# Context tokens of the input projection multiplied in plain float32 from the unsplit weights

## What is computed

```python
hc = modulate(rms_norm(ctx, norm1_g[l]), csh1, csc1)
out_c, ctx_states = mixer_block(hc, lp, (zero_state, zero_state), not last)
hx = modulate(rms_norm(x, norm1_g[l]), sh1, sc1)
out_x, _ = mixer_block(hx, lp, ctx_states, True)
...
def mixer_block(h, lp, init, need_output):
    cb, cc, cx, r, k, v, w_lo, a_lo, g_lo = split_proj(h @ lp["w_in"])
    y, finals = rwkv_scans(r, k, v, w_lo, a_lo, lp, init)
    if not need_output:
        return None, finals
```

## Time and profile before

| | us |
|---|---|
| median of 3 runs | 1660.35 |
| lowest and highest | 1658.63, 1661.67 |
| profiled execution, first to last instruction | 1657.6 |
| TensorE busy in it | 1571.5 |

### The profile page before, as it was taken

How to read it: one execution, slowest core, us unless ns; L and a number is a source line. 1 busy time by engine, 2 the same in 40 slices (tenths; PEclk the granted TensorE clock), 3 DMA queues, 4 the chain that set the end, 5 groups by cost and what they waited for, 6 DMA issues and landing times.

```text
span 1657.6 us, 36556 instructions
## 1 busy us (share of the span) xinstructions
PE 1571.5 (95%) x15540; PEld 1324.2 (80%) x15540; DVE 885.0 (53%) x1417; ACT 572.7 (35%) x987; POOL 219.5 (13%) x230
## 2 busy tenths in 40 slices
PE   7899998999999978999999999999979999999997
PEld 3787886999999766778777887777867788888886
DVE  1624213665566445888887224667454556555222
ACT  3422334332232223434443223535544222323221
POOL 0000002333233010111111121000001011111111
PEclk8899997999999988999999998999979999999999
DMA  8242100332210121222222232221102222222221
GB/s 340 77 147 77 51 26 8 99 106 92 81 42 4 53 77 52 98 79 102 101 81 107 88 104 76 82 79 57 46 26 98 80 93 86 100 101 95 90 102 68
DMA packets 38750, 139.74 MB, mean 84 GB/s; under 512 B 3040, under 2 KB 3552, under 8 KB 38112
## 3 DMA queue, kind: packets, MB, share of 16 engines
q1 hardware_dynamic: 38480, 135.76, 23.4%
q10 hardware_dynamic: 144, 2.10, 0.3%
HBM read 135.75 MB, written 2.10 MB: 83 GB/s over the span
## 4 chain that ended last, share of the span: by engine, by line
PE 86%; DVE 8%; ACT 3%; issue 1%; DMA 0%; POOL 0%; DVEq 0%; SPq 0%; ACTq 0%
PE bank L647 58%; PE bank L780 12%; DVE ffn_sb L2471 2%; PE bank L657 2%; PE bank L967 1%; PE bank L610 1%; PE bank L886 1%; PE bank L908 1%; PE bank L888 1%; PE bank L592 1%; PE bank L1285 1%; PE bank L910 1%; ACT arena L1752 1%; DVE w_in L2091 1%; PE bank L1256 1%
## 5 line engine op out<-in xcount | busy, mean ns | idle before, releaser
L647 PE MATMUL bank<-hf_hi,w_up 128*128 128x512 f32 x1376 | 424.9, 390 | 0.0
L647 PEld LDWEIGHTS bank<-hf_hi,w_up 128*128 128x128 f32 x1376 | 259.1, 188 | 53.6
L647 PE MATMUL bank<-hf_lo,w_up 128*128 128x512 f32 x688 | 271.2, 394 | 4.8 <-DVE w_up L2091 4.3
L647 PE MATMUL bank<-act_hi,w_down 128*128 128x512 f32 x704 | 216.8, 389 | 0.0
L780 PE MATMUL bank<-arena 64*64 64x32 f32 (+2 forms) x4992 | 177.0, 227 | 8.5 <-POOL arena L1930 7.6
L780 PEld LDWEIGHTS bank<-arena 64*64 64x64 f32 x4992 | 170.6, 137 | 13.2 <-issue 8.7
L1403 ACT ACTIVATE w_up<-ring 128x1024 fp32r<-128x1024 f32 x88 | 93.0, 1058 | 215.9 <-PE bank L647 215.9
L2091 DVE TENSOR_TENSOR w_up<-ring,w_up 128x1024 fp32r<-128x1024 f32 x88 | 108.0, 1229 | 105.3 <-ACT w_up L1403 105.2
L647 PEld LDWEIGHTS bank<-hf_lo,w_up 128*128 128x128 f32 x688 | 129.5, 188 | 39.4 <-DVE w_up L2091 13.2
L2471 DVE SCALAR_TENSOR_TENSOR ffn_sb<-ffn_sb 128x512 f32<-128x512 f32 x176 | 151.5, 861 | 5.5
L647 PEld LDWEIGHTS bank<-act_hi,w_down 128*128 128x128 f32 x704 | 132.2, 188 | 27.4
(11 more groups left out here) (319 smaller groups left out, 2364.8 us busy)
## 6 DMA issues: line engine op xcount, KB each, us to landing
ring<-w SPq DMA_DIRECT2D x76, 1024.0 KB, 4.7
ring<-w SPq DMA_DIRECT2D x32, 704.0 KB, 4.0
ring<-w SPq DMA_DIRECT2D x64, 256.0 KB, 2.9
arena<-w SPq DMA_DIRECT2D x2, 3072.0 KB, 22.6
x<-xT SPq DMA_DIRECT2D x1, 2048.0 KB, 11.8
arena<-w SPq DMA_DIRECT2D x2, 1024.0 KB, 20.3
x<-xT ACTq DMA_DIRECT2D x1, 2048.0 KB, 8.9
outT<-x SPq DMA_DIRECT2D x4, 512.0 KB, 2.7
```

Of the source, the lines that this page charges most:

```text
L647: ins = mm(out, w[:, a, k, :], of_block(b, k0 + k), start=first and k == 0 and m == 0, stop=last and k == n - 1 and m == 2)
```

## The change

The context is not split any more. VectorE scales the eight blocks into `hc` in place, ScalarE adds the shift in place (`shifted`) and itself signals `normed`. The nine context products are `whole_product`: eight plain float32 multiplications of 128x256, with the weights taken from the ring's unsplit copy. As TensorE now reads the ring, the slots of `W_INB` and `W_INC` may be loaded over only when the last product of the slot is done: `HELD` gives them `product` in place of `w_lo` in `FREED`. The split of the weights stays, as the x products of the same slots use it; so do all other products.

```diff
+HELD = ("W_INB", "W_INC")
...
+        if _name in WHOLE + HELD:
+            FREED.append(("product", DONE[len(FREED)]))
+        else:
             FREED.append(("w_lo", _n))
-        else:
-            FREED.append(("product", DONE[len(FREED)]))
...
-        hc_ = low_high("hc", at_n + KB * TX, at_s + KB * TX, KB, TC)
...
+            def whole_product(out, w, act):
+
+                for k in range(KB):
+                    ins = mm(out, w[:, k, :], act[:, k, :], start=k == 0, stop=k == KB - 1)
+                ins.then_inc(s["product"], 1)
...
-                        split_product(banks[(base + q * u + c) % (2 * q)][:, 0:t], w_of[name][blk], KB, hi, lo, 0, True, True)
+                        out = banks[(base + q * u + c) % (2 * q)][:, 0:t]
+                        if parts is hc:
+                            whole_product(out, slot_view(SLOT[name] + 2 * i + u)[:, KB * blk:KB * blk + KB, :], hc)
+                        else:
+                            split_product(out, w_of[name][blk], KB, *parts, 0, True, True)
...
-            stage("W_INB", [(0, hx, TX), (1, hx, TX), (1, hc_, TC)], 16)
+            stage("W_INB", [(0, hx, TX), (1, hx, TX), (1, hc, TC)], 16)
...
-            stage("W_INC", [(0, hx, TX), (0, hc_, TC), (1, hx, TX), (1, hc_, TC)], 19, before_last=head_sums)
+            stage("W_INC", [(0, hx, TX), (0, hc, TC), (1, hx, TX), (1, hc, TC)], 19, before_last=head_sums)
...
+            def shifted(shift, whole):
+
+                for k in range(KB):
+                    se.wait_ge(s["h_f"], split_n[0] + k + 1)
+                    act_f(whole[:, k, :], whole[:, k, :], ACT.Identity, bias=shift[:, k:k + 1]).then_inc(s["normed"], 1)
+                split_n[0] += KB
...
-            split_normed(mod[:, 0:8, 1], hc_[0], hc)
+            shifted(mod[:, 0:8, 1], hc)
...
-            norm_split(gains[:, 1], mod[:, 0:8, 1], hc, ctx_sb, rstd_c[:, :], hc_)
+            for k in range(KB):
+                V.scalar_tensor_tensor(hc[:, k, :], ctx_sb[:, k, :], gains[:, 1, k:k + 1], rstd_c[:, :], ALU.mult,
+                                       ALU.mult).then_inc(s["h_f"], 1)
```

More of the change, by code:

```diff
@@ L679, in body @@
                         return
-                    for c, (blk, (hi, lo), t) in enumerate(prods):
+                    for c, (blk, parts, t) in enumerate(prods):
                         pe.wait_ge(s["w_lo"], 4 * i + n0 + 2 * u + blk + 1)
```

## The result

The changed kernel's median is 1664.86 us (1660.42 to 1675.76, 20 runs), that of the kernel before, run beside it, 1659.69 us (1653.61 to 1665.61, 20 runs). The ratio is 1.0041, with a 95% interval of 1.0024 to 1.0057: slower, by 6.8 us from the ratio (4.0 to 9.5), 5.2 from the medians. The prediction said +5.5.

The account below looks back on a forecast made before the run. TensorE was taken to bound the input projection. Nine context products at +0.61 us each gave +5.5 us, VectorE's saving and the ring 0, so 1660.35 became 1665.9 us, with a range of 1662.3 to 1669.2.

Parts of the forecast that it names:

- TensorE bounds the stage: Input projection: TensorE runs its products almost without a hole, so a microsecond more of TensorE is a microsecond more of the whole.
- a sign of being wrong: Behind the input projection: the prediction counts as wrong if what follows the stage does not shift as a block.
- The old product, 2.87 us: Context product before the change: 24 records at 0.1195 us between starts, 0.3586 us a block, 2.87 us for 8 blocks.
- The new product, 3.43 to 3.52 with 3.48 taken: Plain context product, priced from lines 802 and 1049: 0.61 us more than the old, +5.5 us for nine.
- An entry price on top, up to 1.8 us: Start of each plain context product: possibly 0.1 us extra, 0.9 for nine, 1.8 if doubled for a way out.
- VectorE's saving worth 0: VectorE loses eight subtractions while TensorE runs 76.47 us without a wait; the saving was put at 0 us.
- The ring hold worth 0: Ring loads behind W_INB and W_INC wait for the slot's last product; landings of 2.5 to 5.3 us stay covered, 0 us.
- The clock, 1.7 us either way: Two half-clock stretches, after the hole at 155.38 and the head sums: one may be missed or met, 1.7 us either way.
- Four full passes: Rival on the plain product: four passes at the old 0.1195 us each, 3.82 us a product, +8.6 us; chance 0.05.
- Weight loads set the price: Rival on the context products: 0.1195 us is a weight load's price, 16 loads replace 24, -8.6 us; chance 0.04.

## Why the prediction was right

- **TensorE bounds the stage.** Right: the stage grew by the products' 5.2 us, and with a third of the context records gone it shrank by 8.59. What follows did not shift as a block all the way, though, which the prediction named as a sign of being wrong: 6.0 us at `ADA2`, 9.0 at line 1060, 4.9 at the end. The kernel with the longer hold alone, whose stage costs nothing more, scatters there as well (566.40 in place of 564.01 for the records of line 1049, and a span 0.5 us longer), so that sign asked for more than two single profiles can tell. That the span's 4.9 lies near 5.2 is luck in part.
- **The old product, 2.87 us.** Right: 8.59 / 9 = 0.954 for eight records is 0.119 each.
- **The new product, 3.43 to 3.52 with 3.48 taken.** 3.45 measured. The half of line 1049's spacing (0.2144) was a little low and line 802's rounded 0.22 a little high; the truth is 0.2156. The sum came to 5.2 for 5.5.
- **An entry price on top, up to 1.8 us.** There is none: the doubled product shows the second eight at 3.46. The late first start in line 802 does not come back in this stream.
- **VectorE's saving worth 0.** Right as far as the runs can tell: with the work put back TensorE has no new wait and the whole time is the same. The stage's agreement to 0.04 us is chance.
- **The ring hold worth 0.** Right: done alone it leaves the stage at 171.36 us for 171.31.
- **The clock, 1.7 us either way.** The stretches stayed, in 160.00 to 164.00 and around 220 us, and cost about the same: the x products behind the hole and behind the head sums took 7.37 and 7.36 us where a product takes 5.45, 1.9 us each. That such a stretch can be missed or met is seen where VectorE's work was put back: 1.6 us more at one place and 1.6 less at the other. The size of the scatter was low: the head sums alone differ by 2.8 us between two executions.
- **Four full passes** (+8.6). The count fits, as four turns of the columns are 0.427 of the 0.431 us, and the price of one is wrong: 0.1195 is a reduced record with its surplus of 0.013, and a plain multiplication has two records, not four, with next to none. 0.431 is four times 0.108.
- **Weight loads set the price** (-8.6). Half of it may be true. At 128 columns both formats stand at a floor of 0.111 us a record, which fits a weight load, and the old product at 256 columns is just above it. But the plain record at 256 is well over the floor, so having 16 loads in place of 24 buys nothing.

## What to carry to other kernels

With weights of 128x128, three multiplications in the reduced format beat one plain float32 multiplication at 256 columns, 0.359 against 0.431 us. At 128 columns the floor of 0.111 us a record turns it round: a product in two runs took 5.31 us in the reduced format and 3.57 in the plain one. So where tokens are few the plain form is the one to try; where between 128 and 256 columns the two meet was not measured. Price such an exchange by the distance of starts in a running stream of the same width, not by the mean length of a record. Check it in the stage that was changed, not in the difference of two whole spans. And look at what the bounding engine waits for between stages: here waiting for all banks where one was wanted cost as much as the whole change.

## What the runs showed of the hardware that was not expected

A record of 128 columns costs 0.111 us in the reduced format and 0.1116 in the plain one, 93% of what a reduced record of 256 columns costs (0.1195). Halving the columns in two runs therefore made a reduced product 5.31 us instead of 2.87, and a plain one only 3.57 instead of 3.45. The rows of before did not show a floor so near the old price: the head sums in them, 6.92 us for 48 records, ran at half clock in part. At a granted clock of 0.97 they take 0.110 us a record with two columns, so the floor does not depend on the columns. That it is the weight load fits, and was not shown apart from other things that each record has once. Records with narrower weights are shorter, as line 789 with weights of 128x64 and 128 columns in the chain of before, 0.061 us each:

```profile
239.30 1.46 PE bank L789 x24
```

That fits a price of the weights' width as well, but it lies under the 0.107 us of twice the columns too. These multiplications write to one half of the partitions and then the other, so they are no clean test, and what is said above of floor and columns holds for weights of 128x128. The surplus of 0.013 us that a reduced record has above its columns at 256 and at 512 is not explained by any run here.

Besides the stretch at the head sums, the half clock stood behind a wait of TensorE, but not behind the same one in each execution: behind the hole before `W_INC` in the changed kernel (0.62 from 160.00 to 164.00), and behind the wait that ends at 64.47 where VectorE's work was put back (0.82 from 64.50 to 74.00). With the hole before `W_INC` gone it was gone there (1.00 for 0.59).
